# A two-block transformer kernel: the first merge, the output product and the side gate taken as products of rounded parts, and sixteen expert rows computed during the choice

## The chip, the cores and the metric

The kernel runs on one core of a Trainium2 chip. A core has a matrix engine (TensorE, PE in the profile, with its weight loads in the row PEld), a vector engine (VectorE, DVE), a scalar engine (ScalarE, ACT), GpSimd (POOL), and SyncE (SP), from whose queue this kernel starts all its DMA transfers. The five run their own instruction streams and meet by semaphores. The metric is the time of one execution in microseconds (us), lower is better.

## The reference, cut to what matters

Two model blocks are applied to 256 tokens of width 2048. What the change touches:

```python
# first block, after its three branches y_a, y_b, y_c (each 256 x 1024)
merged = mg0 * (y_a @ w_branch[0]) + mg1 * (y_b @ w_branch[1]) + mg2 * (y_c @ w_branch[2])
h = h + merged @ w_out                           # 2048 x 2048
e = rms_norm(p @ w_ple, ple_gain)                # the side input, 256 x 256 @ 256 x 2048
h = h + sigmoid(h @ w_ple_gate) * e              # 2048 x 2048
# second block: x = h; both inputs are normed, then projected
mod = silu(c) @ w_mod + b_mod                    # 2048 x 12288, shifts, scales and gates
h  = rmsnorm(x, norm1_w) * (1 + sc1) + sh1       # 256 tokens
hc = rmsnorm(ctx, norm1_w) * (1 + scc1) + shc1   # 256 context tokens
...                                              # mixer
# experts: 8 heads choose 16 of 16384 each; all experts are computed, with weights that are zero where not chosen
s = top 16 of (q @ sub_keys.T)                   # the choice
act = gelu(h @ u[idx].T)                         # u: 16384 x 2048
y = (softmax(best) * act) @ v[idx]               # v: 16384 x 2048
```

Everything is float32.

## The kernel before, in words

Activations lie transposed: a tile has 128 features on the partitions and the 256 tokens along it, so a width of 2048 is 16 chunks (`DC`). A weight block of 128 output features arrives as one DMA of 1 MB (2048 inputs) or 0.5 MB (1024 inputs, the branch products) in `ring`, four slots of 3072 columns. SP loads block b as soon as block b-4 is used (`weights_used`). `STREAMS` lists the block streams in order: z, window, branch, out, ple, ple_gate, y, l, window2, branch2, out2, peer_q.

There are two ways of making a product. The plain one (`gemm_block`, L311; the branch products, L1508) multiplies float32 tiles; the profile shows two PE instructions for each `nc.tensor.matmul`. The other (`split_products`, L856 to L858; `three_products`, L803 to L805) uses float32r, a type of rounded values: ACT copies the weights rounded (`round_block`, L843), DVE subtracts to get the remainder, in place (`split_block`, L848), and PE adds three products: rounded by rounded, rounded by remainder, remainder by rounded. One `nc.tensor.matmul` is then one PE instruction. ACT rounds block b+2 when block b is used. The z, gate, y and l streams and the experts work so; branch, out, ple, ple_gate, branch2, out2 and peer_q are plain.

*First merge* (`merge_pe`, `merge_dve`): 48 branch blocks of 8 matmuls, three for each of 16 chunks. DVE multiplies each with its gate (L1539) and adds the three (L1543). Behind each chunk DVE also works off two of `MERGE_MODS` = 32 blocks of `w_mod` (`mod_chunk`, L727, a multiply with a sum over 2048 columns). The other 45 of the first 77 are spread over the z stage (`MODS_AT`).

*Out and side gate* (`out_pe`, `out_act`, `out_dve`): 16 blocks of `w_out` over `merged`, added to x (L1557); two blocks of `w_ple`, with four copies of 4 banks' halves to `e` (L1597); the norm of `e` (`norm_act`, `norm_pe`, `norm_dve`: a square over all chunks L329, 16 matmuls with a tile of ones L338, root L331, reciprocal L345, 16 scalings L348); then 16 blocks of `w_ple_gate` over x, each followed by tanh (L1607) and two DVE steps (L1620, L1622) into a second tile that is at last copied over x (L1628).

*Norms of both inputs* (`n2_act`, `n2_pe`, `n2_dve`): first the norm of x, then that of the context, each square, sums, root, reciprocal, scalings; then ACT adds the shift and rounds (L1645), DVE makes the remainders (L1731), and the y stream (20 blocks, both inputs side by side as 512 columns) begins.

*Choice* (`choose_*`): DVE takes the top 16 of each of 32 score rows in 8 rounds, then 4 rounds of combining (`st_cand`), in which ACT does the exponentials (L2732). Then PE turns the indices and the mixed weights (L2761, L2768). `expw_*` builds the weights of all experts and stores them in DRAM in four quarters (L3195). The whole expert input `hp` is then split (ACT L3048, DVE L3109).

*Experts*: 32 groups of 4 rows of 128 experts. A group has a u phase (16 pieces of 512 columns; for each piece 4 matmuls of 512 and 4 of 256 columns, L2977 and L2979), then half-sum, gelu, weighting, rounding and remainder of the 4x256 activations, and a v phase (16 pieces; 6 matmuls of 512 columns each, L3001). The u phase of group g+1 is issued ahead of the v phase of group g. Four piece buffers are rounded by ACT (L3018) and completed by DVE (L3073). u rows live in the ring, one slot each; v rows in one set of four slots (`vslots`), loaded for g+1 when DVE has made the last remainder of group g (`load_v`).

Of the kernel before, what the change touches and what calls it, by code (L numbers as in the profile page):

```python
# [14 lines left out]
P = 128  # L15
# [55 lines left out]
MERGE_MODS = 32  # L71
# [10 lines left out]
def window_order():  # L82
# [14 lines left out]
           ("out", 16, 2048), ("ple", 2, 2048), ("ple_gate", 16, 2048), ("y", N_Y, 2048), ("l", N_L, 2048),  # L97
# [102 lines left out]
def build(nc: bass.Bass, a: dict):  # L200
    with ExitStack() as ctx:
# [36 lines left out]
        Y_ROUNDED = HI_AT + 2 * DC * T + 256  # L238
# [61 lines left out]
        Y_PIECES = GATE_PIECES + 2 * N_GATES  # L300
# [188 lines left out]
        silu3, junk3 = cut(TMP + 4608, D), cut(TMP + 4608 + D, D)  # L489
# [4 lines left out]
        e_at = ZAT + 512  # L494
        e = cut(e_at, DC, T)
        e_sq = cut(e_at + 4096, DC, T)
        e_root = cut(e_at + 8192, T)
        gth = cut(e_at + 8192 + T, SLOTS, T)
        x2 = cut(TMP, DC, T)
# [3 lines left out]
        st_x2 = stage("x2", 1, dve="moved")  # L503
# [19 lines left out]
        sq2 = cut(T2 + 1024, DC, T)  # L523
        root2 = cut(T2 + 5120, T)
        assert T2 + 5120 == L_AT + 4096 + 2 * DC * T
# [3 lines left out]
        KV_TEMPS = HI_AT + 2 * DC * T + 256 + 4096  # L529
        st_hcat = stage("hcat_split", 1, act="m0 m1 m2 m3", dve=" ".join(f"l{c}" for c in range(2 * DC)))  # L530
        st_gain = stage("gain", 1, dve=f"mod0_0 mod0_1 first half_g1 cond_silu mod{N_Z}_0 second", act="cond_tanh")
        st_n2 = [norm_stage("norm2_0", 1, DC, st_e)]
        st_n2.append(norm_stage("norm2_1", 1, DC, st_n2[0]))
        st_shift = stage("shift", 1, act=" ".join(f"shift{c}" for c in range(2 * DC)))
        ctx_loaded = new_sem("ctx_loaded")

        st_cq = norm_stage("norm_cq", 1, 4, st_n2[1])
# [133 lines left out]
        hp_parts, gact_parts, pieces = sb_rounded("hp_parts", 2 * DC * T), sb_rounded("gact_parts", 2 * 2 * GROUP * T), sb_rounded("pieces", NPIECES * 2 * PIECE)  # L671
# [6 lines left out]
        st_hps = stage("hp_split", 1, act="rounded", dve="rest")  # L678
# [61 lines left out]


# [118 lines left out]
        def y_buffer(p):  # L860
            return y_rounded[p % 4]

        def round_y(act, j):
            if j >= 2:
                act.wait_ge(weights_used, streams["y"].first + j - 1)
            round_block(act, streams["y"].first + j, Y_PIECES + 2 * j, y_buffer)

        def split_y(dve, j):
            split_block(dve, streams["y"].first + j, Y_PIECES + 2 * j, y_buffer)
# [628 lines left out]
        def merge_pe(pe):  # L1498
            gate_units(pe, GATES_REST * DC, (N_GATES - GATES_REST) * DC)
            barrier(pe, "fox")  # L1500

            def part(idx, slot, loads, i, u):
                y = YAT[u % 3]
                pe.wait_ge(landed[slot], loads * 16)
                if u >= 4:
                    S["merge"].upto(pe, "dve", f"g{(u - 4) % 3}", (u - 4) // 3)
                for k in range(BC):
                    last = nc.tensor.matmul(bank(4 + u % 4, 0, T), ring[:, slot, k * P:(k + 1) * P], z[:, y + k, :],  # L1508
                                            start=(k == 0), stop=(k == BC - 1))
                last.then_inc(weights_used, 1)  # L1510
            streams["branch"].each(pe, part, step=48)

        def merge_act(act):
            for i in range(GATES_REST, N_GATES):
                keep_gate(act, i)
                if i == N_GATES - SLOTS:
# [3 lines left out]
                    do.end()  # L1520

        def merge_dve(dve):
            for i in range(GATES_REST + 2, N_GATES):
                split_gate(dve, i)
            barrier(dve, "fox")
            do = Do(dve, st_cond, "dve")
# [4 lines left out]
            dve.wait_ge(gates_kept, N_GATES)  # L1531
            for dc in range(DC):
                do, d = Do(dve, st_merge, "dve", dc), merged[:, dc, :]
                if dc:
                    do.own()
                for j in range(3):
                    idx = 3 * dc + j
                    dve.wait_ge(weights_used, streams["branch"].first + idx + 1)
                    do(f"g{j}", nc.vector.scalar_tensor_tensor(out=mtm[:, j - 1, :] if j else d, in0=gate_homes[idx], scalar=1.0, in1=bank(4 + idx % 4, 0, T),  # L1539
                                                               op0=ALU.add, op1=ALU.mult))  # L1540
# [4 lines left out]
                for m in range(2 * dc, 2 * dc + 2):  # L1545
                    mod_chunk(dve, N_Z - MERGE_MODS + m, silu3.rearrange("p (o n) -> p o n", o=1), None)

# [13 lines left out]
        def out_pe(pe):  # L1561
            barrier(pe, "merge")
            gemm(pe, "out", DC, lambda k: merged[:, k, :])

            def ple(idx, slot, loads, i, u):
# [3 lines left out]
                for half_ in range(2):  # L1569
                    if idx or half_:  # L1570
                        do.wait("act", "e0" if half_ else "e1", idx if half_ else idx - 1)
                    for c in range(4):
                        n = half_ * 4 + c
                        for k in range(2):
                            last = nc.tensor.matmul(bank(4 + c // 2, (c % 2) * T, T), ring[:, slot, k * 1024 + n * P:k * 1024 + (n + 1) * P],
# [7 lines left out]
            barrier(pe, "ple")  # L1583
            norm_pe(pe, st_e, 0, e_sq, bank(6, 0, T), DC)
# [1949 lines left out]
```

## Time and profile before

| | us |
|---|---|
| three runs | 4800.66, 4804.59, 4807.0 |
| median | 4804.59 |
| profiled execution | 4805.47 |
| its span, first to last instruction | 4803.6 |
| PE busy | 4322.0 (90%) |
| DVE busy | 2783.6 (58%) |
| ACT busy | 1800.9 (37%) |

The mean granted clock of TensorE is 0.953 of full speed. Records of PE overlap, since matmuls are pipelined: what a matmul costs is read from the length of a run of them over their count, not from the duration of one.

### The profile page before, as it was taken

How to read it: one execution, taken by the hardware profiler on the slowest of the kernel's cores; microseconds unless marked ns; L12 is line 12 of the kernel's file. 1: busy time of each engine (PE TensorE's matmuls, PEld its weight loads, DVE VectorE, ACT ScalarE, POOL GpSimd, SP SyncE). 2: the span in 40 equal slices, each digit the busy share in tenths (PEclk: the TensorE clock that was granted, in tenths of full speed). 3: DMA queues.
4: the chain of work that ended last, by engine and by line, in shares of the span. 5: the costliest groups of instructions: out<-in, count | busy, mean ns of one | idle time of the engine just before them, and what ended most of it. 6: DMA issues, size and time to landing. Idle time of an engine off the chain costs nothing.

```text
span 4803.6 us, 63190 instructions
## 1 busy us (share of the span) xinstructions
PE 4322.0 (90%) x25888; PEld 3784.6 (79%) x25888; DVE 2783.6 (58%) x4560; ACT 1800.9 (37%) x2924; POOL 0.2 (0%) x4
## 2 busy tenths in 40 slices
PE   6999789999878998879998998367999999999997
PEld 5999668988767885668887987356888888888886
DVE  6878735562127754457775200586666666666665
ACT  3444454400113242344433101055545555555553
POOL 0000000000000000000000000000000000000000
PEclk9999999999999999989998999778999999999998
DMA  6777342496343442200003443114454455455452
GB/s 250 293 294 301 123 149 97 151 353 241 114 166 141 183 165 72 84 16 1 1 1 123 148 184 107 61 43 184 181 214 194 189 223 201 178 217 210 187 199 88
DMA packets 135606, 759.84 MB, mean 158 GB/s; under 512 B 12209, under 2 KB 29745, under 8 KB 66097
## 3 DMA queue, kind: packets, MB, share of 16 engines
q1 hardware_dynamic: 135344, 756.13, 41.9%
q8 instruction: 192, 3.15, 0.3%
q14 instruction: 70, 0.57, 0.0%
HBM read 735.11 MB, written 20.97 MB: 157 GB/s over the span
## 4 chain that ended last, share of the span: by engine, by line
PE 61%; DVE 8%; ACT 3%; issue 1%; DMA 0%; DVEq 0%; SPq 0%; ACTq 0%
PE ps L3001 14%; PE ps L2977 10%; PE ps L311 7%; PE ps L2979 5%; PE ps L856 3%; PE ps L858 3%; PE ps L857 3%; PE ps L2680 2%; PE ps L2916 1%; PE ps L2489 1%; PE ps L2492 1%; PE ps L2908 1%; PE ps L2480 1%; PE ps L338 1%; DVE ring_rounded L848 1%
## 5 line engine op out<-in xcount | busy, mean ns | idle before, releaser
L2977 PE MATMUL ps<-hp_parts,pieces 128*128 128x512 f32 x2048 | 728.9, 400 | 33.3 <-DVE pieces L3073 33.3
L3001 PE MATMUL ps<-pieces,gact_parts 128*128 128x512 f32 x3072 | 706.2, 391 | 5.3 <-issue 2.8
L3001 PEld LDWEIGHTS ps<-pieces,gact_parts 128*128 128x128 f32 x3072 | 576.5, 188 | 126.7 <-DVE pieces L3073 3.6
L2979 PE MATMUL ps<-hp_parts,pieces 128*128 128x256 f32 x2048 | 577.0, 282 | 0.0
L805 PE MATMUL ps<-x_rounded,ring_rounded 128*128 128x256 f32 x2000 | 560.1, 280 | 0.0
L3073 DVE TENSOR_TENSOR pieces<-ring,pieces 128x512 fp32r<-128x512 f32 x512 | 353.7, 692 | 309.0 <-ACT pieces L3018 309.0
L2977 PEld LDWEIGHTS ps<-hp_parts,pieces 128*128 128x128 f32 x2048 | 387.1, 189 | 129.7 <-issue 25.7
L3018 ACT ACTIVATE pieces<-ring 128x512 fp32r<-128x512 f32 x512 | 323.8, 634 | 399.5 <-PE ps L2979 312.4
L3073 DVE TENSOR_TENSOR pieces<-area,pieces 128x512 fp32r<-128x512 f32 x512 | 352.9, 690 | 161.9 <-ACT pieces L3018 153.2
L3018 ACT ACTIVATE pieces<-area 128x512 fp32r<-128x512 f32 x512 | 322.6, 631 | 312.2 <-PE ps L3001 200.8
L2979 PEld LDWEIGHTS ps<-hp_parts,pieces 128*128 128x128 f32 x2048 | 389.1, 190 | 1.2
L805 PEld LDWEIGHTS ps<-x_rounded,ring_rounded 128*128 128x128 f32 x2000 | 379.6, 190 | 0.0
L311 PE MATMUL ps<-area,ring 128*128 128x256 f32 x1536 | 336.8, 383 | 26.5 <-ACT area L2719 15.7
L803 PE MATMUL ps<-x_rounded,z_rounded 128*128 128x256 f32 x1232 | 345.8, 281 | 15.8 <-DVE hn_rest L828 15.8
L311 PEld LDWEIGHTS ps<-area,ring 128*128 128x128 f32 x1536 | 294.8, 192 | 68.5 <-issue 26.3
L804 PE MATMUL ps<-hn_rest,z_rounded 128*128 128x256 f32 x1232 | 348.0, 282 | 0.0
L856 PE MATMUL ps<-x_rounded,ring_rounded 128*128 128x256 f32 x832 | 245.2, 295 | 17.6 <-DVE ring_rounded L848 17.5
L803 PEld LDWEIGHTS ps<-x_rounded,z_rounded 128*128 128x128 f32 x1232 | 231.9, 188 | 16.2 <-issue 16.2
L803 PE MATMUL ps<-x_rounded,ring_rounded 128*128 128x256 f32 x768 | 225.2, 293 | 21.2 <-DVE ring_rounded L909 20.9
L857 PE MATMUL ps<-hcat_rest,ring_rounded 128*128 128x256 f32 x832 | 238.5, 287 | 0.0
L858 PE MATMUL ps<-x_rounded,ring_rounded 128*128 128x256 f32 x832 | 238.0, 286 | 0.0
L804 PEld LDWEIGHTS ps<-hn_rest,z_rounded 128*128 128x128 f32 x1232 | 232.0, 188 | 0.0
(446 smaller groups left out, 7484.4 us busy)
## 6 DMA issues: line engine op xcount, KB each, us to landing
ring<-u_dram SPq DMA_DIRECT2D x128, 1024.0 KB, 6.8
area<-v_dram SPq DMA_DIRECT2D x128, 1024.0 KB, 8.7
ring<-w_mod_dram SPq DMA_DIRECT2D x96, 1024.0 KB, 7.1
ring<-w_mg_dram SPq DMA_DIRECT2D x80, 1024.0 KB, 4.8
ring<-w_z_dram SPq DMA_DIRECT2D x77, 1024.0 KB, 4.9
ring<-w_branch_dram SPq DMA_DIRECT2D x80, 512.0 KB, 4.3
ring<-w_out_dram SPq DMA_DIRECT2D x32, 1024.0 KB, 4.8
ring<-w_y_dram SPq DMA_DIRECT2D x20, 1024.0 KB, 4.8
```

What stands on the lines that cost most here:

```text
L311: last = nc.tensor.matmul(bank(slot, 0, n) if out is None else out, ring[:, slot, k * P:(k + 1) * P], rhs(k), start=(k == 0), stop=(k == k ...
L803: nc.tensor.matmul(out, rounded, hn_rounded[:, k, :], start=first, stop=False)
L804: nc.tensor.matmul(out, rounded, hn_rest[:, k, :], start=False, stop=False)
L805: return nc.tensor.matmul(out, rest, hn_rounded[:, k, :], start=False, stop=last)
L856: nc.tensor.matmul(out, w, rounded, start=(k == 0), stop=False)
L857: nc.tensor.matmul(out, w, rest, start=False, stop=False)
L858: return nc.tensor.matmul(out, w_rest, rounded, start=False, stop=(k == DC - 1))
L2977: both = nc.tensor.matmul(bank(s).rearrange("p (a t) -> p a t", t=T), piece[:, b, 0, k * P:(k + 1) * P], hp2[:, :, c, :], start=(c == 0), ...
L2979: last = nc.tensor.matmul(bank(s, 0, T), piece[:, b, 1, k * P:(k + 1) * P], hp2[:, 0, c, :], start=False, stop=(c == DC - 1))
L3001: last = nc.tensor.matmul(out, gact[:, k, ga, s, t * P:(t + 1) * P], piece[:, b, va, :], start=(s == 0 and w == 0), stop=(s == GROUP - 1 a ...
L3018: nc.scalar.activation(piece[:, n % NPIECES, 0, :], source, ACT.Copy).then_inc(rounded, 1)
L3073: nc.vector.tensor_tensor(piece[:, b, 1, :], source, piece[:, b, 0, :].bitcast(F32), ALU.subtract).then_inc(remainders, 1)
```

## The change

- `MERGE_MODS` falls from 32 to 25. 52 `w_mod` blocks are then worked off in the z stage, 13 in the merge (one behind the first gate product of a chunk, for chunks 2 to 14) and 12 in the out stage, one for each of the blocks 0 to 11.
- The branch, out and ple_gate streams use three products of rounded parts. The branch inputs are split in six steps among the last gates, `merged` and the new x chunk by chunk.
- ple comes ahead of out. The sums of the norm of `e` are issued behind out block 1, its scalings in blocks 4 to 11.
- The context norm lies inside the ple_gate blocks, with shift and remainder; the squares and sums of x follow block by block; DVE and ACT then interleave scaling, shift and remainder of x by chunks. The gate's result goes to x directly.
- The u products of groups 0 to 3 are plain float32 products on PE during the choice, with their gelu at once; the results lie in x, which is first stored and later loaded back. In the expert stage the u phase of group 4 comes first, then v phases 0 to 3 in direct succession, then as before.
- The split of `hp` is made in four quarters, and only the last waits for the store of the expert weights; the zeroing of the accumulator moves behind the first remainders.

```diff
-MERGE_MODS = 32
+MERGE_MODS = 25
+MERGE_MODS_AT = [6 + 3 * n for n in range(13)] + [48 + n for n in range(12)]
+MERGE_LOADS_AT = [0, 1] + [n + 1 for n in MERGE_MODS_AT[:-2]]
...
+            for u in range(3 * DC):                                   # merge_pe
+                at, j = streams["branch"].first + u, u % 3
...
+                pe.wait_ge(weights_split, BRANCH_PIECES + u + 1)
+                out = bank(4 + u % 4, 0, T)
                 for k in range(BC):
...
+                    nc.tensor.matmul(out, w, branch_in[j][:, k, :], start=(k == 0), stop=False)
+                    nc.tensor.matmul(out, w, branch_rest[:, j, k, :], start=False, stop=False)
+                    last = nc.tensor.matmul(out, w_rest, branch_in[j][:, k, :], start=False, stop=(k == BC - 1))
...
                     do(f"g{j}", nc.vector.scalar_tensor_tensor(...))   # merge_dve
+                    if idx + 2 < 3 * DC:
+                        split_branch(dve, idx + 2)
+                    if j == 0:
+                        merge_mods(dve, idx)
+                    if j == 1 and dc:
+                        merged_remainder(dve, rest, dc - 1)
...
+            for b in range(3 * DC):                                   # merge_act, behind the last keep_gate
+                round_branch(act, b)
...
         def out_act(act):
+            round_run(act, 0)
             barrier(act, "fox", "merge")
             # the four copies of ple; round_run(act, 1) behind the first two
...
+            for b in range(DC):                                       # out_dve
+                dve.wait_ge(weights_used, streams["out"].first + b + 1)
+                nc.vector.scalar_tensor_tensor(out=xc[:, b, :], ...).then_inc(evacuated, 1)
+                merge_mods(dve, 3 * DC + b)
+                split_run(dve, b + 2)
+                x2_remainder(b)
...
+                if 4 <= b < 12:                                       # two scalings of e
...
+            for c in range(DC + 1):                                   # the norm of x, out_dve
+                if c < DC:
+                    norm(f"scaled{c}", ...)
+                if c:
+                    S["shift"].upto(dve, "act", f"x{c - 1}", 0)
+                    split(f"l{c - 1}", ...)
...
+            split_run(dve, 2 * DC + 1)
...
+            for g in range(EARLY):                                    # choose_pe, EARLY = 4
+                for r in range(GROUP):
+                    pe.wait_ge(u_landed[r], g * 16 + 16)
...
+                    for c in range(DC):
+                        last = nc.tensor.matmul(bank(GROUP * (g % 2) + r, 0, T), ring[:, r, c * P:(c + 1) * P], hp[:, c, :], ...)
+                    last.then_inc(early_made, 1)
+            pe.wait_ge(early_kept, EARLY)
             barrier(pe, "scores", "cand")
...
+        def has_u(g):
+            return EARLY <= g < NG - 1
...
-            u_pe(pe, 0, 0)
+            u_pe(pe, EARLY, 0)
             def group(g, k):
-                if not is_last(g):
-                    u_pe(pe, g + 1, base(g))
+                if has_u(g):
+                    u_pe(pe, g + 1, u_base(g + 1))
...
-            do("rounded", nc.scalar.activation(hp2[:, 0, :, :], hp, ACT.Copy))   # experts_act
+            for q in (1, 2, 3, 0):
+                if q == 0:
+                    act.wait_ge(w_stored[1], 32)
+                do(f"r{q}", nc.scalar.activation(hp2[:, 0, 4 * q:4 * q + 4, :], hp[:, 4 * q:4 * q + 4, :], ACT.Copy))
```

## Rows read from the trace of the kernel before

**Rows 1.** The profile's page: busy time of each engine.
```profile
PE 4322.0 (90%) x25888; PEld 3784.6 (79%) x25888; DVE 2783.6 (58%) x4560; ACT 1800.9 (37%) x2924; POOL 0.2 (0%) x4
```
**Rows 2.** Windows: start:end, length, busy (count) per engine, PE clock, DMA share, GB/s.
```profile
952.00:1118.00 166.00, 166.00 (x775) 146.24 (x774) 98.00 (x137) 0.47 (x1) 0.00 (x0) 1.00 0.92 339
1118.00:1129.00 11.00, 1.17 (x5) 0.77 (x4) 5.78 (x7) 0.00 (x0) 0.00 (x0) 0.76 1.00 423
1129.00:1241.00 112.00, 112.00 (x509) 98.11 (x509) 6.37 (x15) 0.00 (x0) 0.00 (x0) 0.98 0.46 164
1241.00:1284.00 43.00, 25.56 (x102) 20.55 (x100) 8.60 (x18) 10.75 (x8) 0.00 (x0) 0.84 0.19 74
1284.00:1396.00 112.00, 112.00 (x511) 98.31 (x512) 12.77 (x30) 5.77 (x15) 0.00 (x0) 0.98 0.40 141
1396.00:1456.00 60.00, 19.68 (x67) 15.52 (x65) 31.03 (x62) 29.14 (x44) 0.00 (x0) 0.68 0.37 140
```
**Rows 3.** Windows of the z stage, the delta-rule stage and the experts.
```profile
100.00:440.00 340.00, 340.00 (x2889) 340.00 (x2889) 273.75 (x242) 142.75 (x180) 0.00 (x0) 1.00 0.78 295
...
2160.00:2500.00 340.00, 328.30 (x2565) 280.06 (x2565) 257.11 (x574) 154.26 (x394) 0.00 (x0) 1.00 0.01 1
...
3357.00:4772.00 1415.00, 1408.26 (x7072) 1192.04 (x7072) 949.69 (x1364) 712.62 (x1097) 0.00 (x0) 1.00 0.50 193
```
**Rows 4.** Timeline of the merge, DVE: start, length, instruction, [idle before].
```profile
963.39 0.42 DVE L1539 SCALAR_TENSOR_TENSOR area<-area,ps 128x256 f32<-128x256 f32 x1 [3.03 <-PE ps L1508]
963.85 0.89 DVE L1543 TENSOR_TENSOR area<-area 128x256 f32<-128x256 f32 x2
964.65 2.29 DVE L727 SCALAR_TENSOR_TENSOR ring<-ring,area 128x2048 f32<-128x2048 f32 x1
```
**Rows 5.** Timeline between ple and the y stream.
```profile
1256.44 3.72 PE L1575 MATMUL ps<-p,ring 128*128 128x256 f32 x16 [1.17 <-ACT area L1597]
...
1442.96 3.90 ACT L843 ACTIVATE y_rounded<-ring 128x1024 fp32r<-128x1024 f32 x4
1444.91 4.63 DVE L848 TENSOR_TENSOR ring_rounded<-ring,y_rounded 128x1024 fp32r<-128x1024 f32 x4
...
1449.45 12.76 DVE L1731 SCALAR_TENSOR_TENSOR hcat_rest<-area,mod,hcat_rounded 128x256 fp32r<-128x256 f32 x32
...
1456.33 0.79 PE L856 MATMUL ps<-hcat_rounded,y_rounded 128*128 128x512 f32 x1 [20.15 <-DVE hcat_rest L1731]
```
**Rows 6.** DMA issues: transfer, count, size, median us from issue to landing.
```profile
ring<-w_branch_dram SPq DMA_DIRECT2D x80, 512.0 KB, 4.3
ring<-w_out_dram SPq DMA_DIRECT2D x32, 1024.0 KB, 4.8
...
x<-x_dram SPq DMA_DIRECT2D x2, 2048.0 KB, 9.7
```
**Rows 7.** Timeline of the choice: PE's last work ahead of it and first behind it.
```profile
3042.24 7.41 PE L2752 MATMUL ps<-misc,area 128*128 128x128 f32 x64 [0.58 <-ACT area L1685]
...
3164.57 1.09 PE L2761 MATMUL ps<-consts,area 128*128 128x128 f32 x4 [114.91 <-DVE area L2855]
```
**Rows 8.** Timeline from the last expert weights to the second u phase.
```profile
3300.51 0.32 SPq L3195 DMA_DIRECT2D experts_dram<-area  x1
...
3311.68 3.62 ACT L3048 ACTIVATE hp_parts<-area 128x4096 fp32r<-128x4096 f32 x1 [11.19 <-DMA experts_dram<-area]
...
3324.81 0.77 PE L2977 MATMUL ps<-hp_parts,pieces 128*128 128x512 f32 x1 [25.49 <-DVE pieces L3073]
...
3356.83 0.80 PE L2977 MATMUL ps<-hp_parts,pieces 128*128 128x512 f32 x1 [7.76 <-DVE pieces L3073]
```
**Rows 9.** Timeline of the last v phase, which follows a v phase directly.
```profile
4738.64 4.50 PE L3001 MATMUL ps<-pieces,gact_parts 128*128 128x512 f32 x12 [2.83 <-issue]
...
4747.28 10.06 PE L3001 MATMUL ps<-pieces,gact_parts 128*128 128x512 f32 x36 [2.04 <-DVE pieces L3073]
...
4766.90 1.28 DVE L3098 TENSOR_TENSOR area<-area,ps 128x512 f32<-128x512 f32 x2 [3.55 <-PE ps L3001]
```

More of the change, by code:

```diff
@@ L1608, in out_act @@
-            streams["ple_gate"].each(act, gate)
+                if idx == 0:
+                    round_run(act, 1)
+            norm = Do(act, st_e, "act")
+            norm("squares", nc.scalar.activation(e_sq, e, ACT.Square))
+            x2 = Do(act, st_x2, "act")
+            for b in range(DC):
+                round_run(act, b + 2)
+                if b == 1:
+                    norm.wait("pe", "sums")
+                    norm("root", nc.scalar.activation(e_root, bank(0, 0, T), ACT.Sqrt, bias=par("eps"), scale=1.0 / D))
+                    norm.end()
+                act.wait_ge(evacuated, evacuated_from["out"] + b + 1)
+                x2(f"r{b}", nc.scalar.activation(x2_rounded[:, b, :], xc[:, b, :], ACT.Copy))
@@ new lines, in out_act @@
+            x_square(act, n2, DC - 1)
+            n2.wait("pe", "sums")
+            n2("root", nc.scalar.activation(root2, bank(4, 0, T), ACT.Sqrt, bias=par("eps"), scale=1.0 / D))
+            n2.end()
+            round_run(act, 2 * DC + 1)
+            for c in range(DC):
+                S["norm2"].upto(act, "dve", f"scaled{c}", 0)
+                shift(f"x{c}", nc.scalar.activation(hcat_rounded[:, 0, c, :], hcat[:, 0, c, :], ACT.Identity, bias=modv[:, c, 0:1]))
+            shift.end()
@@ L1623, in gate @@
                 do.end()
[L1624 to L1646 removed]
+                if i + 1 < DC:
+                    split_run(dve, DC + i + 2)
@@ new lines, in out_dve @@
+                if i == 5:
+                    norm.wait("act", "root")
+                    norm("inverse", nc.vector.reciprocal(root2, root2))
+                    norm.own()
+                if 5 <= i < 13:
+                    for c in (2 * (i - 5), 2 * (i - 5) + 1):
+                        norm(f"scaled{c}", nc.vector.scalar_tensor_tensor(out=hcat[:, 1, c, :], in0=hcat[:, 1, c, :], scalar=gain1v[:, c, 1:2], in1=root2, op0=ALU.mult, op1=ALU.mult))
+                if 7 <= i < 15:
+                    for c in (2 * (i - 7), 2 * (i - 7) + 1):
+                        ctx_remainder(c)
@@ L1647, in n2_act @@
+            norm.end()
+            split.end()
+            split_run(dve, 2 * DC + 1)
+            y_dve(dve, gain)
+        def n2_act(act):
             do = Do(act, st_gain, "act")
@@ L3129, in group @@
                         add(dve, g, n // GROUP - 1)
-                    if n == 4 and not is_last(g):
+                    if n == 4 and has_u(g):
                         sum_halves(dve, g + 1)
```

469 lines of the change are left out of this document (310 added, 159 removed).

## The prediction

> **What bounds the kernel now.** I read the busy shares on the profile's page first: PE is busy in 90% of the span, DVE in 58%, ACT in 37% [rows 1]. The chain that ended last says the same: it stays on PE except for a few stretches. So I ask two things: which PE work is made shorter, and which of PE's idle stretches go. The windows show them. The merge is 166.0 us of plain float32 matmuls at full clock, with the DMA engines 92% busy; then come about 10 us with hardly a matmul, out at 112 us, 43 us with PE busy in 25.6, the side gate at 112 us, and 60 us with PE busy in 19.7 [rows 2]. The choice has a PE gap of 114.9 us [rows 7]. Ahead of the experts lie gaps of 25.5 and 7.8 us [rows 8]. The experts themselves are PE from end to end, 1408 of 1415 us at clock 1.00 [rows 3].
>
> **Prices.** A plain float32 matmul of 256 columns is two instructions; 511 of them fill 112.0 us [rows 2], so 0.438 us a matmul. One product of rounded parts: 2889 instructions in 340.0 us [rows 3], 0.1177 us, so three make 0.353 us. Ratio 0.806. DVE: gate product 0.42 us, two adds 0.89, one `w_mod` block 2.29 (2.37 with its read of the sum) [rows 4]; remainder of 1024 columns 4.63 / 4 = 1.16, of 256 columns 12.76 / 32 = 0.40; ACT rounds 1024 columns in 3.90 / 4 = 0.98 [rows 5].
>
> **Z stage.** It takes 7 more `w_mod` blocks of 2.37 us of DVE each, 17 us over about 435. DVE is busy 273.75 of 340 there and DMA 0.78 [rows 3]; with 7 MB more the DMA share is about 0.82. Slots and rounding run two blocks ahead. Cost 0; if that cover fails, at most the 17 us.
>
> **Merge.** 48 x 8 x 3 = 1152 instructions x 0.1177 = 135.6 us if PE sets the pace, 8.47 us a chunk. DVE per chunk: 3 x 0.42 + 3 x 1.16 + 2.37 + 0.40 + 0.89 = 8.40 us, before any wait. The two are level, so in the 13 chunks with a `w_mod` block I take 8.65: 138 us. Ends: 135.6, and 152 if waits bring DVE to 9.5 a chunk. DMA falls from 3.7 MB in 10.4 us to 2.6 MB in 8.6, no bound; a branch block has two block times, 5.65 us, less 0.98 for rounding, to land in, against 4.3 [rows 6]. New at the start: `round_branch(0)` stands behind the last `keep_gate` on ACT, which waits for PE's last gate. Gate kept 0.47, rounded 0.98, remainder 1.16, some semaphores: PE idles 3 us. After: 141 us for 166. **Gain 25.**
>
> **From the last branch product to the first side-gate product.** Before: 1118.8 to 1283.9, 165.1 us. The 9.8 us wait is for out's first block, which stood behind three `w_mod` loads and x. After: ple first. Its weights are loaded in time, but `round_run(0)` stands ahead of ple's copies on ACT and waits for out block 0, which stands behind x (2 MB, 9.7 us [rows 6]) in the queue: about 7.5 us after the last branch product. ACT rounds (2.0), then copies ple's first half at 9.5 to 10.5; PE, with two halves of 3.7 us [rows 5] done at 7.2, waits 3.4 us, and ple ends at about 18. Ends 15 and 24.
>
> Out: PE needs 48 x 0.1177 = 5.65 us a block. DVE per block: 0.42 + 2.37 + 2 x 1.16 + 0.40 = 5.5 us, and 0.8 more for two scalings in blocks 4 to 11: 6.3 to 6.45 with semaphores. That is over 5.65, so DVE sets the pace there. A second loop gives nearly the same: the `w_mod` block for out block 2+k is loaded behind out block 5+k, after block 1+k is used; two 1 MB loads land 7.6 us later (4.8 for one alone [rows 6]), then 2.37 and 2.32 us of DVE must be over before block 4+k: 12.3 us over two blocks, 6.15 each. Block by block: blocks 0 and 1 at 5.65; the sums of `e` behind block 1, 16 x 0.44 = 7.0 us; then up to block 12 about 6.4 us each; the last three at 5.65. Sum 106 us, end at 18 + 106 = 124. Ends: 97 (PE alone) and 120. **Gain 165 - 124 = 41**, in which the norm of `e` (23.7 us between ple and the side gate before) has shrunk to its sums.
>
> **Side gate.** 16 x 5.65 = 90.4 us, plus 16 context sums and 14 of x in between, 30 x 0.44 = 13.2: 103.6 for 112.6. DVE has 0.9 + 2.3 + 0.8 + 0.8 = 4.8 us a block, ACT 0.4 + 2.0 + 0.4 + 0.8 = 3.6, both under 5.65. **Gain 9.**
>
> **To the second y block.** Before: 1396.5 to 1456.33, then y block 0 in 13.6 us, its start at low clock: 73.5 us. After the last side-gate product: tanh, two DVE steps, square, sum, root, reciprocal (1.75), first scaling, shift and remainder, about 7.3 us. Then DVE makes a scaling and a remainder per chunk, 0.82 us, 15 times: 12.3, with y block 0 running behind. Then the remainder of y block 1 (2.3) stands last in DVE's queue and block 1 waits for it: 22.5 us. Ends 19 and 32. **Gain 51.**
>
> **Choice.** 4 x 4 x 16 = 256 plain matmuls x 0.438 = 112 us on PE. They start at 3049.7, behind the score products [rows 7], and end at 3162; the choice ends at 3164.57. They fit by 1 to 2 us, so they are free only as long as DVE's choice takes its 115 us; each us over that is paid. u rows need 1 MB in 7 us. ACT's four gelus fall between the exponentials. Since PE no longer rests, the turns and first weight products behind it run at full clock: +2 (ends 4 and -5). **Gain 2.**
>
> **Start of the experts.** Before: last weights stored at 3300.51, ACT begins at 3311.68, PE at 3324.81 [rows 8]. After: three quarters of `hp` are rounded during the store; behind it one quarter (1.06), its remainder (1.22), one piece (0.69): PE starts at 3314.7, 10.1 earlier. The zeroing, weighting and splitting of group 0 then stand on DVE ahead of the half-sum of group 4: 6.7 us gap where 7.76 was. **Gain 11.**
>
> **Expert loop.** A u phase has 64 x (512 + 256) columns and a v phase 96 x 512: both 49152. The window holds 31 u and 32 v phases and one late transition: (1415 - 8.8) / 63 = 22.3 us a phase [rows 3]. Four u phases leave: 89.3. But v phases 0 to 3 now follow each other directly, with one set of v slots, filled only when the last remainder of the group before is made. The trace has this case once, at the end: idle from 4735.8, products from 4738.64, end 4766.9, the first 12 at 0.375 us apiece [rows 9], so 31.1 us for a phase of 22.3, 8.8 lost. Three transitions: 26.4. Ends: 5 us each (only the idle, 2.83 + 0.4 + 2.04) and 13. **Gain 63.**
>
> **Sum.** 25 + 41 + 9 + 51 + 2 + 11 + 63 = 202. 4805.5 (profiled execution; 0.9 above the median of the runs) - 202 = 4603.5; with a little for waits not seen, **4605**.
>
> **A rule against it.** In the delta-rule stage PE waits a little between groups of matmuls, 11.7 us of 340 in all, and the clock stays at 1.00 [rows 3], its level of 2.4 GHz; after the one long wait among the v phases the matmuls take 0.375 us for 0.22, the level of 1.2 GHz [rows 9]. The Trainium skill, TensorE: Matmul & The Clock Gate, section A second HAM failure mode: psum-queue depth-cycling, says that frequent short waits between matmul groups can make the clock swing between its two levels. By that rule out and the y start, where PE waits for DVE at every block, would swing; by the row of the delta-rule stage they do not. My sum follows the row.
>
> **The rivals.**
> - *DVE is the bound of the merge and out, well beyond my 8.65 and 6.4 us.* For: the sums of its work are level with or over PE's, and every wait adds. Against: the z stage runs DVE at 0.81 without a stall. Price: merge +14, out +8, y start +5: 4632. Chance 0.17.
> - *DVE keeps up, and the v transitions cost only their idle.* Merge -2, out -6, v -11: 4586. Chance 0.13.
> - *The choice gets longer or its cover fails*: u rows late, or a gelu ahead of an exponential. For: only 1 to 2 us of slack. Price 10 to 25: 4623. Chance 0.07.
> - *The clock swings in the stretches paced by DVE.* For: the page above. Against: [rows 3]. If out and a third of the merge run at 1.2 GHz, PE needs 90 us and 45 us more: about 4720. Chance 0.04.
> - *Slower than before: in the whole expert loop the clock falls.* PE no longer rests in the choice, and if those rests are what the later clock lives on, the loop would run partly at half speed. A phase costs 22.3 us more at 1.2 GHz; from nine such phases of the remaining 60 the gain of 202 is gone. With half of them it is 4605 + 669 = 5274. Against: 1415 us at 1.00 without rest. Chance 0.02.
> - My forecast, 4592 to 4620: the remaining 0.57.
>
> **Range and chances.** 4580 to 4640 takes in the second, third and fourth case and the bounds of merge, out and transitions one at a time, and leaves out about 0.17. What can be told from no change here is about 0.2%, 10 us; all but the last rival are far below. Faster 0.97, same 0.01, slower 0.02.
>
> **What would show it.** In the profile after: branch products in about 138 us behind a 3 us gap; a wait of PE in ple on ACT's copy; out blocks 6.4 us apart with PE waiting for the remainders of weights; side gate about 104; the y stream beginning some 8 us after the side gate; no PE gap in the choice and the turn of the indices at the same distance from the scores; PE starting 14 us after the last expert store; three gaps among the first v phases, each followed by slow matmuls. It is wrong if out runs at 5.65 or above 7 us a block, if the v transitions differ from 8.8 by more than 4 us each, or if PE's early products end behind the choice.

## The result, and the profile after

The changed kernel takes 4608.71 us (median of 4 runs, 4606.63 to 4609.68) where the kernel before takes 4804.33 (4800.66 to 4807.0): ratio 0.9593, 95% interval 0.9576 to 0.9609. The forecast was 4605, range 4580 to 4640. The profiled execution took 4608.16, its span is 4606.4.

The page, as [rows 1] was of before, and its chain of waits by engine:

```profile
PE 4275.7 (93%) x26784; PEld 3780.7 (82%) x26784; DVE 2876.4 (62%) x4644; ACT 1897.9 (41%) x3029; POOL 0.2 (0%) x4
...
PE 80%; DVE 10%; ACT 4%; DMA 3%; issue 1%; SPq 0%; DVEq 0%; ACTq 0%
```

PE has 896 instructions more and 46 us less of busy time: three short products stand where one slow one stood. The windows, as [rows 2] and [rows 3]: merge, ple, out, side gate, the step to y, y block 0, the early products, the first v phases, the expert loop.

```profile
954.40:1106.20 151.80, 141.89 (x1153) 140.16 (x1154) 119.32 (x166) 54.12 (x61) 0.00 (x0) 0.98 0.79 270
1106.00:1126.90 20.90, 15.76 (x65) 13.29 (x64) 6.42 (x8) 7.27 (x8) 0.00 (x0) 0.84 0.62 261
1127.00:1229.00 102.00, 100.47 (x804) 98.23 (x803) 79.66 (x101) 42.15 (x49) 0.00 (x0) 1.00 0.72 268
1229.00:1333.20 104.20, 104.15 (x827) 102.40 (x827) 66.16 (x101) 55.00 (x84) 0.00 (x0) 1.00 0.50 182
1333.20:1340.40 7.20, 1.78 (x6) 0.61 (x5) 4.21 (x7) 5.65 (x9) 0.00 (x0) 0.78 0.85 296
1340.40:1362.00 21.60, 21.58 (x86) 17.41 (x87) 19.19 (x34) 14.42 (x19) 0.00 (x0) 0.92 0.60 234
2931.70:3042.30 110.60, 110.60 (x515) 97.19 (x513) 101.19 (x564) 16.90 (x25) 0.00 (x0) 1.00 0.49 176
3240.00:3270.00 30.00, 24.69 (x106) 19.16 (x105) 19.39 (x29) 11.31 (x19) 0.00 (x0) 1.00 0.41 158
3340.00:4530.00 1190.00, 1190.00 (x6011) 1008.85 (x6011) 805.03 (x1152) 609.47 (x939) 0.00 (x0) 1.00 0.52 200
```

Each row is start:end, length, busy (count) of PE, its weight loads, DVE, ACT and POOL, granted clock, DMA share, GB/s. Two windows have PE well short of busy with its clock near full: the merge, where 10 us of 151.8 are waits, and the first v phases, where 5.3 of 30 are. From out to the last side-gate product PE is dense. The granted clock is low in ple (0.84), in the 7 us ahead of y (0.78) and at the start of y (0.92 over 21.6 us). From first starts and last ends of PE's groups in both traces, the spans divide so (us):

| stretch | before | after | gain | predicted |
|---|---|---|---|---|
| start to last gate | 953.0 | 951.4 | 1.6 | 0 |
| to the last branch product | 165.8 | 154.6 | 11.2 | 25 |
| to the first side-gate product | 165.1 | 122.8 | 42.3 | 41 |
| side gate | 112.6 | 104.2 | 8.4 | 9 |
| to the first product behind y | 288.9 | 235.6 | 53.3 | 51 |
| to the first score product | 1356.8 | 1355.9 | 0.9 | 0 |
| to the first expert weight | 133.7 | 135.4 | -1.7 | 2 |
| to the first u product | 148.9 | 138.0 | 10.9 | 11 |
| to the last v product | 1441.7 | 1370.2 | 71.5 | 63 |
| to the end | 37.1 | 38.3 | -1.2 | 0 |
| sum | 4803.6 | 4606.4 | 197.2 | 202 |

The sum is right within 5 us, but two terms miss by more than that in opposite directions, the merge by 14 and the loop by 8.5. That the total came so close is in good part luck. The experiments are about these two first, then about what I had called free.

### The profile page after: what moved, and what is told of

It reads as the page before. It is cut to its first block, busy times and chain, and to the rows that moved or that the text cites. A ratio compares the mean times of both kernels' runs of the same rounds, so it can differ in the third digit from the quotient of the medians.

```text
span 4606.4 us, 64970 instructions
## 1 busy us (share of the span) xinstructions
PE 4275.7 (93%) x26784; PEld 3780.7 (82%) x26784; DVE 2876.4 (62%) x4644; ACT 1897.9 (41%) x3029; POOL 0.2 (0%) x4
## 4 chain that ended last, share of the span: by engine, by line
PE 80%; DVE 10%; ACT 4%; DMA 3%; issue 1%; SPq 0%; DVEq 0%; ACTq 0%
PE ps L3222 14%; PE ps L3198 9%; PE ps L320 5%; PE ps L822 5%; PE ps L3200 5%; PE ps L824 5%; PE ps L823 5%; PE ps L875 4%; PE ps L877 4%; PE ps L876 4%; PE ps L2868 2%; PE ps L2677 1%; PE ps L3126 1%; PE ps L2680 1%; PE ps L3118 1%
## 5 line engine op out<-in xcount | busy, mean ns | idle before, releaser
L3198 PE MATMUL ps<-hp_parts,pieces 128*128 128x512 f32 x1792 | 635.5, 399 | 15.3 <-DVE pieces L3294 15.3
L824 PE MATMUL ps<-x_rounded,ring_rounded 128*128 128x256 f32 x2000 | 564.2, 282 | 0.0
L3200 PE MATMUL ps<-hp_parts,pieces 128*128 128x256 f32 x1792 | 503.7, 281 | 0.0
L3294 DVE TENSOR_TENSOR pieces<-ring,pieces 128x512 fp32r<-128x512 f32 x448 | 309.7, 692 | 268.7 <-ACT pieces L3239 268.7
L3239 ACT ACTIVATE pieces<-ring 128x512 fp32r<-128x512 f32 x448 | 282.9, 632 | 342.9 <-PE ps L3200 264.3
L3198 PEld LDWEIGHTS ps<-hp_parts,pieces 128*128 128x128 f32 x1792 | 337.4, 188 | 99.3 <-issue 15.5
L3200 PEld LDWEIGHTS ps<-hp_parts,pieces 128*128 128x128 f32 x1792 | 339.2, 189 | 1.1
L877 PE MATMUL ps<-x_rounded,ring_rounded 128*128 128x256 f32 x1088 | 310.2, 285 | 0.0
L875 PE MATMUL ps<-x_rounded,ring_rounded 128*128 128x256 f32 x832 | 244.8, 294 | 17.6 <-DVE ring_rounded L867 17.5
L822 PE MATMUL ps<-x_rounded,ring_rounded 128*128 128x256 f32 x768 | 225.7, 294 | 21.2 <-DVE ring_rounded L945 20.9
L320 PE MATMUL ps<-area,ring 128*128 128x256 f32 x1024 | 223.4, 381 | 16.7 <-ACT area L2907 15.7
L320 PEld LDWEIGHTS ps<-area,ring 128*128 128x128 f32 x1024 | 195.8, 191 | 44.3 <-issue 16.1
```

The lines of the kernel that those rows point to most:

```text
L320: last = nc.tensor.matmul(bank(slot, 0, n) if out is None else out, ring[:, slot, k * P:(k + 1) * P], rhs(k), start=(k == 0), stop=(k == k ...
L822: nc.tensor.matmul(out, rounded, hn_rounded[:, k, :], start=first, stop=False)
L824: return nc.tensor.matmul(out, rest, hn_rounded[:, k, :], start=False, stop=last)
L875: nc.tensor.matmul(out, w, rounded, start=(k == 0), stop=False)
L877: return nc.tensor.matmul(out, w_rest, rounded, start=False, stop=(k == DC - 1))
L3198: both = nc.tensor.matmul(bank(s).rearrange("p (a t) -> p a t", t=T), piece[:, b, 0, k * P:(k + 1) * P], hp2[:, :, c, :], start=(c == 0), ...
```

## The merge: which queue

What the chain of waits of the changed kernel's merge holds (share by line, then start, length and line of its longest pieces):

```profile
by line: DMA ring<-w_branch_dram 36.1%; PE ps L1548 17.4%; PE ps L1550 16.4%; PE ps L1549 16.3%; DMA ring<-w_out_dram 8.0%; DVE ring_rounded L905 5.9%; ACT ring_rounded L900 5.1%; issue 1.0%
...
964.68 8.30 DMA ring<-w_branch_dram
973.00 1.07 ACT ring_rounded L900
974.09 1.24 DVE ring_rounded L905
975.47 0.35 PE ps L1548
...
992.65 7.28 DMA ring<-w_branch_dram
...
1011.23 8.67 DMA ring<-w_branch_dram
```

The chain goes seven times from PE to a load of a branch block that takes 6.4 to 8.7 us, through its rounding and its remainder, back to PE. I had given such a block 5.65 us less the rounding, against the 4.3 us of [rows 6], where the landing of every branch block goes into one median. The other candidate is DVE, which has about as much work in a chunk as PE. So the loads and DVE's products were made small, one at a time and together.

**e1** leaves the loads small:

```diff
-                load_mod(sp, m, m)
+                sp.wait_ge(mod_used, m - 1)
+                n = 64 if m >= N_Z - MERGE_MODS + 2 else 1024
+                sp.dma_start(mod_slots[m % 2][:, :, 0:n], a["w_mod"][m].rearrange("p (b n) -> p b n", b=2)[:, :, 0:n]).then_inc(mod_landed[m % 2], 16)
```

> The w_mod loads of merge and out are cut to 128 of 2048 columns (all but the first two); DVE works on full blocks as before, so the last coefficients are computed from old data and the output is not the reference's. Theory A (a branch block that is loaded right behind a 1 MB w_mod block lands 6.4 to 8.7 us after its issue, later than PE wants it): merge 151.6 -> 137 to 141 us. Rival B (DVE's own work in a chunk is more than the 8.65 us I took, and sets the pace of the merge): merge stays 149 to 152. Out: if DVE sets its pace (my step) it stays 100 to 102; if the loop over the w_mod loads sets it, 101.9 -> about 97. Whole kernel 4608.7 -> 4594 to 4598 by A, 4605 to 4609 by B.

**e2** leaves the products small:

```diff
+                k, v = MOD_ORDER[n], mod_slots[n % 2][:, :, 0:32]
...
+                done = nc.vector.scalar_tensor_tensor(out=v, in0=v, scalar=1.0, in1=silu3[:, 0:64].rearrange("p (b n) -> p b n", b=2),
+                                                      op0=ALU.mult, op1=ALU.mult, accum_out=modv[:, k, 0:1])
```

> The w_mod blocks of merge and out are loaded in full, but DVE multiplies only 64 of their 2048 columns, 0.1 to 0.2 us for 2.3 (output not the reference's). Theory A (late branch loads): merge stays 148 to 152. Rival B (DVE sets the pace): merge 151.6 -> 136 to 139. Out: if DVE sets its pace, 101.9 -> 97 to 98 (16 x 5.65 and 7 of sums); by the loop over the w_mod loads, 99 to 102. Whole kernel about 4604 by A, about 4590 by B.

**e9** does both.

> e1 and e2 together: small w_mod loads and small w_mod products in merge and out (output not the reference's). Theory H (the merge's excess over PE's 135.6 us is a chain of both: the branch block lands late and its remainder then stands behind a w_mod block on DVE; each alone gives back most of it, what is left in either is the other's): first to last branch product 136 to 137.5 us for 140.2 and 142.3, out kept 92 to 93 us from first to last. Rival (a third cause, such as PSUM or ACT, holds the last 4 us): 139.5 or more.

**e3** keeps all the work and splits the loads:

```diff
+            for b in range(2):
+                at = step - b
+                if at in MERGE_LOADS_AT and 6 < at < 43:
...
+                    load_mod_half(sp, m, m, b)
```

> Every w_mod block is loaded as two halves of 0.5 MB; in the merge the second half is issued one branch block later, so that no branch load stands behind more than 0.5 MB. Same work everywhere. Theory A: branch loads land 1.2 us earlier, near 5.5 us after issue; merge 151.6 -> 139 to 143, whole kernel 4608.7 -> 4597 to 4601. Rival B (DVE): merge within 1 us of 151.6, whole kernel 4607 to 4610.

Measured from the first branch product to the start of the last: changed kernel 151.5 in its profile, and 145.8 to 147.7 in four other kernels with the same merge (e4, e5, e6, e7), so the profile that I read first was the worst of five. e1 140.3, e2 142.3, e9 137.8, e3 143.4. Whole kernels: e1 4592.79, e2 4597.92, e9 4591.04 (two runs), e3 4605.76. What PE waited for in the merge, in the changed kernel, e1, e2 and e3 (total us, times, longest); 3.0 us of each are the gap at the start:

```profile
PE ps L1548 <- DVE ring_rounded L905: 12.9, 10, 3.0
...
PE ps L1550 <- DVE ring_rounded L907: 3.7, 2, 3.0
...
PE ps L1548 <- DVE ring_rounded L905: 5.7, 7, 3.0
...
PE ps L1559 <- DVE ring_rounded L916: 4.8, 2, 3.0
```

DMA rows of the merge, 960 to 1090 us (median us from issue to landing), changed kernel, e1:

```profile
ring<-w_branch_dram SPq DMA_DIRECT2D x41, 512.0 KB, 5.5
ring<-w_mod_dram SPq DMA_DIRECT2D x13, 1024.0 KB, 7.8
```

```profile
ring<-w_branch_dram SPq DMA_DIRECT2D x44, 512.0 KB, 3.5
...
ring<-w_mod_dram SPq DMA_DIRECT2D x13, 64.0 KB, 3.1
```

Theory B is out: it said that e1 would stay at 149 to 152. In e1 DVE has all its work (busy 119.2 us, as in the changed kernel), and PE waits no more than in e9, 3.7 us; what e1 is longer than e9 lies in the matmuls themselves, 139.9 us of PE for 137.4, and stays unexplained. Theory A met its range in e1 (137 to 141) and missed in e2, where it said 148 to 152. So the late loads are what the waits need, and DVE's `w_mod` product, 2.3 us in front of the remainder of the late block, makes them longer: with full loads and small products 2.7 us of waits remain beyond the start, with both full 5 to 10. Theory H, a chain with both links, holds in that sense. e9's 137.8 lies a little over its 137.5 and well under the rival's 139.5; its first 17 or so matmuls, behind the gap at the start, run at the lower clock, so a little of it is that.

Later profiles say the same of e3. Four kernels with halved `w_mod` loads in the merge (e3, e8, and e10 and e12 of a later section) have a merge of 140.7 to 143.4 us; six with whole loads have 145.8 to 151.5. The sixth is e11, also of that section, which has whole loads and only 9 blocks there for 13: 150.9 us, with 13.1 us of waits. Fewer blocks did not shorten it, smaller loads did. That e3's whole kernel gained only 3 us (expected by theory A 8 to 12) has a reason ahead of the merge: e3 halves the loads of the z stage as well, where PE then waited 2.9 us between 100 and 440 us and the changed kernel not at all.

The first profile has one thing more. Behind a wait of 2.13 us at 1022 the matmuls of the changed kernel go on at the lower clock; the 20 us around it were granted 0.94 and 0.89, where e4 to e7 show 1.00.

Out was tested by the same runs. DVE's first to last evacuation, changed kernel, e1, e2:

```profile
L1786 DVE SCALAR_TENSOR_TENSOR x<-ps,x x16: 359/418/426, 1133.0 to 1229.0; 128x256 f32<-128x256 f32 x16
```

```profile
L1788 DVE SCALAR_TENSOR_TENSOR x<-ps,x x16: 360/420/426, 1121.7 to 1215.4; 128x256 f32<-128x256 f32 x16
```

```profile
L1795 DVE SCALAR_TENSOR_TENSOR x<-ps,x x16: 360/424/426, 1126.5 to 1219.2; 128x256 f32<-128x256 f32 x16
```

96.0 us, then 93.7, 92.7, and 92.6 in e9; 15 blocks of 5.65 and 7 us of sums are 91.8. (e4 to e7 give 95.9 to 96.2.) So PE very nearly sets out's pace: 5.93 us a block, not my 6.4. With DVE's work whole and the loads small, 1.1 of the 3.4 us over e9 are left; with the loads whole and the products small, 0.1. DVE's sum of work, which I had named as the bound, is therefore not it. What both cuts fit is the second loop of the prediction, through a `w_mod` load and the DVE steps behind it, which either cut makes shorter; it costs 3.4 us, not the 9 by which my 106 stood over PE's 97. From its first product to the first of the side gate, out took 99.6 us in e1 and 98.5 in e2, in both between the two ranges that had been set against each other.

## The expert loop: what a direct transition costs

PE's timeline over v phases 0 to 3 of the changed kernel, which follow each other directly; [rows 9] shows the one such place of before:

```profile
3229.20 24.72 PE L3222 MATMUL ps<-pieces,gact_parts 128*128 128x512 f32 x96 [7.11 <-DVE pieces L3294]
3256.68 1.63 PE L3222 MATMUL ps<-pieces,gact_parts 128*128 128x512 f32 x6 [2.77 <-issue]
3259.14 1.65 PE L3222 MATMUL ps<-pieces,gact_parts 128*128 128x512 f32 x6 [0.83 <-DVE pieces L3294]
3261.62 1.66 PE L3222 MATMUL ps<-pieces,gact_parts 128*128 128x512 f32 x6 [0.83 <-DVE pieces L3294]
3264.16 17.98 PE L3222 MATMUL ps<-pieces,gact_parts 128*128 128x512 f32 x78 [0.88 <-DVE pieces L3294]
3285.37 2.20 PE L3222 MATMUL ps<-pieces,gact_parts 128*128 128x512 f32 x6 [3.22 <-issue]
...
3313.58 4.54 PE L3222 MATMUL ps<-pieces,gact_parts 128*128 128x512 f32 x12 [2.72 <-issue]
```

The three gaps are there. But behind the first the matmuls go on at full clock (six in 1.63 us), and only behind the second and third do they start slow (six in 2.20 us, 0.367 apiece, and 12 in 4.54 us, 0.378 apiece, the level of 1.2 GHz; what went before was 3 us of idle as in the first). I had copied all of [rows 9], idle and slow start, three times.

**e4** gives the v rows a second set of slots, and loads group g+2 when group g is done:

```diff
-        vslots = cut(0, GROUP, D)
+        vslots = [[cut(0, GROUP, D)[:, s:s + 1, :] for s in range(GROUP)],
+                  [cut(12288, 3, D)[:, s:s + 1, :] for s in range(3)] + [(ring[:, 3, D:], cut(18432, 1024))]]
...
-                    load_v(g + 1)
+                    load_v(g + 2)
```

> A second set of v slots (three in free memory, the fourth in two halves), v rows of group g+2 loaded when group g is done. Theory C (between v phases that follow each other PE waits for v rows that can be loaded only after the last remainder before, 2.7 to 3.2 us and then 0.4 to 0.9 for each next row, and part of the clock): from the first v product to the first u product of group 5 109.7 -> 91 to 93 us, and at the end the last v phase starts without a gap, 5 to 8 us: whole kernel 4608.7 -> 4582 to 4587. Rival D (the v phases are longer for themselves, through the additions on DVE and ACT's rounding when no u phase lies between): 109.7 -> 103 or more, whole kernel 4600 to 4605.

Measured: 4584.40 (4575.26 to 4588.18), ratio 0.9536 [0.9520, 0.9552]. Its timeline for the same four phases is one row:

```profile
3239.10 90.05 PE L3224 MATMUL ps<-pieces,gact_parts 128*128 128x512 f32 x384 [7.12 <-DVE pieces L3299]
```

90.05 us for 109.7, a little under the 91 to 93 expected: theory C. The three early transitions cost 19.65 together, 6.6 each. The one at the end, from the start of v phase 30 to the last v product, goes from 52.9 to 43.7, 9.2 for my 8.8. D is out: without the gaps a v phase is 22.5 us long, so ACT and DVE keep up.

**e7** is e4 with the start mended: zeroing (in two halves), weighting and splitting of group 0 among the pieces of u phase 4, the half-sum of group 4 among those of v phase 0.

```diff
+                if n in (2, 5):
+                    dve.wait_ge(w_stored[0], 32)
+                    nc.vector.memset(yacc[:, n // 4, :], 0.0).then_inc(zeroed, 1)
+                if n == 8:
+                    weigh(dve, 0, 0)
+                if n == 12:
+                    split_gact(dve, 0, 0)
```

> e4_two_v, and in it zeroing, weighting and splitting of group 0 and the half-sum of group 4 stand among the pieces of u phase 4 and v phase 0, as they do for all later groups. Theory G (the 7.1 us wait ahead of the first v phase is DVE's queue): the gap goes to 0 to 1.5 us, and with it the low clock of v phase 0, whole kernel 4584.4 -> 4575 to 4579. Rival: the 3.5 us of zeroing among the pieces make PE wait in u phase 4 for as long, gain 0 to 3.

Measured: 4569.43 (4564.82 to 4570.06), 15 less than e4 and more than the 5 to 9 expected. Window from its first u product into v phase 3:

```profile
3194.60:3308.00 113.40, 113.38 (x525) 94.92 (x526) 90.68 (x128) 57.18 (x89) 0.00 (x0) 0.99 0.66 261
```

PE does not stop once, so the 7.1 us gap was DVE's queue, and the zeroing hides among the pieces. From first u to last v product e4 takes 1341.2 and e7 1331.1, so the edit is worth 10: the 7.1 us gap, and some 3 us of low clock behind it (in the changed kernel, with the same gap, v phase 0 took 24.72 us, where a phase at full clock takes 21.95). The profiles differ by 13 us more ahead of the experts, where the two kernels are the same (their first u products start at 3207.8 and 3194.6), and e4's four runs spread over 13 us. So the 5 us by which the medians differ beyond 10 need not be the edit's.

## One part undone, and the order in ple

**e5** is the front half of the changed kernel with the choice and the experts of before.

> The front half of the changed kernel (merge, out, side gate, norms) with the choice and the experts of the kernel before: the part 'four groups' first products in the choice' undone alone. By my sum (choice 2, start 11, loop 63) it costs 76 us: 4685. By the landmarks of the traces (135.4 for 133.65, 138.0 for 148.9, 1370.2 for 1441.7, some 1 us behind) about 80: 4687 to 4691. Theory E (the early products and their gelus lengthen the choice): from the first score product to the first weight product 133.5 to 134. Rival (the 1.7 us come with the other data or place of the choice): 135 to 135.5. Nothing may change before the scores: if the parts add up, they lie 117 to 118 us earlier than in the kernel before, as in the changed one.

Measured: 4690.12 (4687.28 to 4692.15), ratio 0.9767 [0.9750, 0.9783]. So the early groups are worth 81.4 us and the rest 114.2; the expectation by the trace's landmarks, 4687 to 4691, was met, and the one by my sum, 4685, was 5 us short. The scores lie 117.8 us earlier than in [rows 7], as in the changed kernel. Their rows, scores and first weight products in e5, then in the changed kernel:

```profile
2924.49 7.41 PE L2937 MATMUL ps<-misc,area 128*128 128x128 f32 x64 [0.58 <-ACT area L1893]
3048.55 1.09 PE L2946 MATMUL ps<-consts,area 128*128 128x128 f32 x4 [116.64 <-DVE area L3040]
...
3059.86 1.41 PE L3093 MATMUL ps<-area 128*128 128x128 f32 x5 [4.53 <-DVE area L3075]
```

```profile
2924.54 7.41 PE L2951 MATMUL ps<-misc,area 128*128 128x128 f32 x64 [0.58 <-ACT area L1896]
3048.62 1.09 PE L2971 MATMUL ps<-consts,area 128*128 128x128 f32 x4 [6.16 <-DVE area L3065]
3059.93 1.41 PE L3118 MATMUL ps<-area 128*128 128x128 f32 x5 [4.53 <-DVE area L3100]
```

The two agree within 0.1 us, so theory E is wrong: the choice is 1.7 us longer than in [rows 7] also without an early product in it. It is spread evenly over DVE's eight rounds: from the third on they begin about 7.6 us apart, where those of the kernel before begin 7.37 apart. What makes it so in both kernels stays open. The early products themselves fill 110.6 of the 116.6 us and cost nothing in the choice. My +2 for a warm clock behind them is wrong too: PE idles 6.2 us and 4.5 us there, and the first five weight products take the same 1.41 us as in e5.

**e6** moves one call on ACT:

```diff
-            round_run(act, 0)
             barrier(act, "fox", "merge")
...
-                if idx == 0:
-                    round_run(act, 1)
+                round_run(act, idx)
```

> ACT rounds out's first block behind its copies of the first ple block, not ahead of them. Theory F (PE waits in ple for the copy because ACT waits for out's first block, which lands behind x): ple 20.9 -> 14.5 to 16 us, out starts as soon, whole kernel 4608.7 -> 4602 to 4604. Rival: out's first block is then late by the same time (it lands 7.5 us after the last branch product, is rounded 2.0 and split 1.2 us later), and from the last branch product to the first side-gate product 122.8 stays within 1 us.

Measured: 4601.44 (4596.33 to 4603.66), ratio 0.9583 [0.9567, 0.9599]. PE's ple rows, changed kernel and e6:

```profile
1106.01 7.07 PE L1661 MATMUL ps<-p,ring 128*128 128x256 f32 x32
1118.22 9.08 PE L1661 MATMUL ps<-p,ring 128*128 128x256 f32 x32 [5.14 <-ACT area L1719]
```

```profile
1102.42 13.98 PE L1661 MATMUL ps<-p,ring 128*128 128x256 f32 x64
```

20.9 becomes 13.6 (ahead of theory F's 14.5, because the second half no longer starts at low clock), and out starts at once behind it. Last branch product to first side-gate product is 7 us shorter, so the rival (122.8 us stay) is out.

## What I had called free: the z stage

**e8** puts e3, e4, e6 and e7 together.

> e3, e4, e6 and e7 together. If the parts add up: 4608.7 - 3 to 8 (halved w_mod loads) - 24 to 29 (two sets of v slots) - 5 (ple) - 7 (start of v) = 4560 to 4570. If the merge's gain is given back behind it, 4568 to 4575.

Measured: 4558.97 (4555.22 to 4562.96), ratio 0.9496 [0.9480, 0.9512]: 50 us less than the changed kernel and the best version here. It missed its range by 1 us on the good side; the medians' steps of e3, e4 to e7, and e6 (3, 39 and 7 us) add up to it. Inside it something is paid back: with the loads halved in out too, DVE's evacuations span 99.3 us there (96.9 in e3) for 96.0.

**e10** and **e11** move seven more `w_mod` blocks from merge and out to the z stage, e10 in e8, e11 in the changed kernel alone; **e12** moves three in e8 and halves loads only in the merge.

```diff
-MERGE_MODS = 25
-MERGE_MODS_AT = [6 + 3 * n for n in range(13)] + [48 + n for n in range(12)]
+MERGE_MODS = 18
+MERGE_MODS_AT = [6, 9, 15, 18, 24, 27, 33, 36, 42] + [48, 49, 50, 51, 53, 55, 57, 59, 61]
```

> e8_all, and seven more of the w_mod blocks of merge and out go into the z stage (18 stay, 9 in the merge, 9 in out). By the sums: merge -2 to -3, out -3 (seven times 2.37 us less on DVE, of which out's share counts where DVE sets the pace), z stage DVE about 0.91 and DMA about 0.90 of the time, no stall: 4559 -> 4552 to 4555. Rival: the z stage is then over its edge (z blocks land late behind more w_mod blocks), its 340 us grow by 3 or more, and the kernel is at 4558 or above.

> The changed kernel with 18 w_mod blocks in merge and out for 25, the other seven in the z stage, loaded whole, and nothing else. Theory I (a loop in the z stage: SP waits until DVE has used a w_mod block, the z block behind it lands late, ACT rounds it late, DVE comes late; seven more blocks put it over its edge): the gates end 35 to 45 us later than in the changed kernel, merge and out are 6 shorter, 4608.7 -> 4637 to 4648. Rival (the halved loads of e10, which raised the landing of a z block from 6.5 to 7.2 us in e8, are the cause): the gates end within 5 us of the changed kernel, 4600 to 4606.

> e8_all with 22 w_mod blocks in merge and out (11 and 11), three more in the z stage, and halved loads only in the merge, whole ones in z as in the changed kernel. If the edge of the z stage lies beyond 55 blocks: merge and out 2 to 3 us shorter, 4559 -> 4555 to 4558. If 55 blocks are already over it: 4560 to 4575.

Measured: e10 4593.86, 35 more than e8; e11 4638.83, 30 more than the changed kernel; e12 4562.01, 3 more than e8, which is within the spread of their runs (4560.25 to 4567.21 and 4555.22 to 4562.96). Three more blocks brought no gain where 1 to 4 us were expected, and the stage shows why: from 100 to 440 us e12's PE does 57 matmuls fewer than the 2889 of e8 and of the changed kernel, some 7 us, and has waited 3.8 us. In e11 the gates end 34 us later than in the changed kernel (35 to 45 expected), in e10 41 later than in e8. So the count is the cause, theory I, and the halved loads are not the main one; the further 7 us of e10, and the 2.9 us of waits in e3, leave them a share. e10's own expectation was wrong by 39 us. What the DMA queue itself waits for, 100 to 440 us, before, changed kernel, e11 (total us, times, longest):

```profile
SPq L3233 <- PE ps L805: 273.9, 60, 5.3
SPq L717 <- DVE ring L730: 22.9, 10, 2.5
```

```profile
SPq L3470 <- PE ps L824: 155.0, 51, 5.3
SPq L731 <- DVE ring L744: 110.9, 28, 8.5
SPq L731 <- DVE ps L741: 25.9, 11, 6.3
```

```profile
SPq L731 <- DVE ring L744: 207.9, 28, 11.2
SPq L731 <- DVE ps L741: 75.3, 15, 8.0
SPq L3470 <- PE ps L824: 1.4, 4, 0.5
```

When SP waits for PE, the next z block is issued as soon as its slot is free, so that wait served here as a measure of the slack. Seven blocks took it from 274 to 155 us at no cost; seven more took it to 1, and the chain of waits of e11 runs through the z loads (40.7%), DVE's remainders and products (43.9%) and ACT's rounding (5.0%), with PE at 7%: the loop of theory I. In e12, three blocks more than in the changed kernel, it is down to 4.5 us already. With halved loads it was 105.7 us in e8 and 36.0 in e3, which have the same z stage, so near the edge one profile says little. The busy shares hold nothing of that: DVE's 273.75 of 340 and a DMA share of 0.78 [rows 3] became 292.5 and 0.85 in the changed kernel, and in e11 they are 282.5 and 0.78, with the stage slower.

## Why the prediction was right, and where not

- **Merge, 25 forecast, 11.2 measured.** The mis-sized term is "a branch block has two block times, 5.65 us, less 0.98 for rounding, to land in, against 4.3". Right behind a `w_mod` load the branch block takes 6.4 to 8.7, and with DVE's product behind it the merge is 146 to 151.5 us, not 138. The 135.6 us of PE and the 3 us gap at the start were near (e9: 137.8; gap 3.0). The first rival (DVE beyond 8.65 us a chunk, merge +14) had the size but not the cause: in e1 DVE had all that work and PE hardly waited.
- **Last branch product to side gate, 41 and 42.3.** Right as a sum; inside it, two errors cancel: ple took 20.9 for 18 and out 102 for 106. PE waited in ple 5.1 us on ACT's copy, for the reason given; e6 takes it away. In out the step "DVE sets the pace there" failed: the blocks came 5.93 us apart, near the 5.65 that I had named as a sign of being wrong, and e1 shows that DVE's work alone costs about 1 us.
- **Side gate, 9 and 8.4; start of y, 51 and 53.3.** y began 7.4 us behind the side gate, forecast 7.3. Block 1 of y did not wait for its remainder: the window 1340.4 to 1362 has PE busy in 21.58 of 21.6.
- **Choice, 2 and -1.7.** The products fitted, as said. The warm clock behind them didn't come, and 1.7 us stay open.
- **Start of the experts, 11 and 10.9.** The gap ahead of v phase 0 was 7.1 for 6.7.
- **Expert loop, 63 and 71.5.** The mis-sized term is the price of a transition, 8.8, taken from one place: 6.6 each for three, so 7 of the 8.5 us. The place at the end itself costs 9.2.
- **z stage, 0 and 0.** Right, but for a reason that I had not looked at. The DMA share rose to 0.85 for my 0.82, and the shares of DVE and DMA gave no warning that the next seven blocks cost 30 to 35 us.
- **The clock.** Out and the merge, which waits in places, ran at 1.00 and 0.98. The Trainium skill (TensorE: Matmul & The Clock Gate, section A second HAM failure mode: psum-queue depth-cycling) warns of a swing behind frequent short waits. In this trace the merge fell to the lower level once, behind the wait of 2.13 us, and came back; out did not fall. So [rows 3] decided rightly against a price of over 100 us. That price was itself not added up right: 90 and 45 us on 4605 are 4740, not 4720. The expert loop stayed at 1.00 from 3340 to 4530 us without its rest in the choice.

## What to carry to other kernels

Price a load by what is issued right ahead of it on its queue, not by the median of its kind; and where work is moved into a full stage, look at what the DMA queue waits for: while it waits for the bound engine there is room, and when it waits for the engine that got the work there is none. When two queues could be the cause, cut each alone and both together, and read the waits and not only the total: here the loads were what the waits needed, and the vector engine's product made them longer. A price taken from a single place in a trace deserves a range, since the clock behind a wait of the same length was once full and once half.

## What the hardware showed that I had not expected

- Waits of 2.77, 3.22 and 2.72 us between v phases: behind the first PE went on at full clock, behind the other two at the lower level for 12 matmuls or so. Behind the fourth direct transition, at the end, 2.64 us of wait were followed by full clock again (six matmuls in 1.62 us), while in the merge a wait of 2.13 us, and in e3 one of 1.87 us, were followed by the lower level. The length of the wait alone did not decide it.
- The same code in front of the merge ended its gates anywhere from 951.4 to 961.6 us in the profiles of e4, e5, e6, e7 and the changed kernel, with the granted clock of 600 to 750 us between 0.88 and 0.94. Comparisons of single profiles are therefore made by stage, not by time from the start.
